# Value products of attention behind every second unit, block 2's latent half ahead of the shift, and a variance sum moved to VectorE

## The chip, the cores and the metric

One core of one Trainium2 chip runs the whole program in one launch. The metric is the device time in microseconds (us); the number that counts is the median of three runs. TensorE (PE in the profile) does the matrix products, VectorE (DVE) and ScalarE (ACT) the elementwise work, GpSimd (POOL) some sums and descriptors, SyncE (SP) issues most transfers.

## The reference

Two layers of a hybrid backbone over 512 latent and 256 context tokens of width 1024. A modulation vector (6 x 1024 wide, from `silu(c) @ w_ada`) gives shift, scale and gate.

```python
h = modulate(rmsnorm(x, g_mix[l]), sh1, sc1)
hc = modulate(rmsnorm(ctx, g_mix[l]), csh1, csc1)
q, k, v, u = split_in(h @ w_in[l])                 # 8 query heads, 2 key/value heads, and the conv columns u
a_out = latent_attention(q, k, v, k_c, v_c, attn_sink[l])   # window of +/-128 tokens, all context keys, a sink
cv_out = conv_module(u, w_dw[l], b_dw[l], ln_g[l], ln_b[l]) # GLU, 31 taps, layernorm, silu
x = x + gt1 * merge_groups(a_out, cv_out, g_attn_out[l], g_conv_out[l], w_out[l])
h2 = modulate(rmsnorm(x, g_ffn[l]), sh2, sc2)
x = x + gt2 * swiglu(h2, w_gate_up[l], w_down[l])
...
mu = jnp.mean(xf, axis=-1, keepdims=True)          # layernorm of the conv branch
var = jnp.mean(jnp.square(xf - mu), axis=-1, keepdims=True)
y = (xf - mu) * lax.rsqrt(var + EPS)
```

Context tokens go through the same weights in the first layer; in the second only their keys and values are needed.

## The kernel before, in words

Activations lie with features on the 128 partitions and tokens along the free axis. Every weight and activation is split into a high and a low part, and each product is made of three matrix products (high x high, high x low, low x high). ScalarE makes the high part of a 128x1024 weight block (line 989), VectorE the low part (line 1327). The order on each engine is written out by hand and tied together by semaphores; there is no planner.

**The start (lines 860 to 905).** The first phase, `u`, has eight blocks of output columns (four pairs). The RMS root is applied after the product, so products can start with `gain * x`. TensorE first makes the scale half of the first modulation group (`first_unit(0, k)`, eight units of four products each, fed by 1 MB transfers that hold two units), with filler products (`keep_busy`) between. Then it makes the latent half of block 0 and block 1 (`latent_part`, 512 columns), with the eight units of the shift half between, turns the shift's row (`first_turn(1)`), waits for the shift (`sh_ok`), and makes the context half of both blocks (`context_part`, 256 columns and the two shift columns). Blocks 2 to 7 are made whole by `gemm_block` in `phase`, with the units of the second modulation group (`ada_unit`, 1 MB each, two buffers) between, and two conv tiles. The loads of these stand on SP's queue, in order, each behind a semaphore that says that its buffer is free.

**The normalisation of the conv branch.** ScalarE squares the centred tiles (`dev_ok`), GpSimd adds the four squares (lines 1921 to 1925), TensorE turns the sum (`var_tokens`, in block 3 of phase `qkv`), VectorE reduces it and inverts ScalarE's root (`diagonal`), and TensorE broadcasts it in block 4.

**Attention (lines 735 to 850, 1070 to 1110, 1424 to 1505).** A unit is one head of one 128-query block; four units make a group (one KV head, one query block), which has 4, 5, 5, 4, 2 or 2 key tiles by its query block (in the second layer 4, 5, 5, 4). In unit n TensorE turns the probabilities of n (`turn`, line 800, into the one bank pair `PTB`), makes the scores of unit n + 4 (line 787, two banks in turn), and part of the value products of the group before (`values`, line 815: two products of 64 output rows, at two places of the array). ScalarE copies the turned probabilities (`prob_turned`, line 1090) and then takes the exponential of unit n + 3 (line 1080). VectorE takes the maximum of unit n + 4 and divides unit n + 2. Three waits matter here:

```python
pe.wait_ge(pt_ok, u)       # turn(n): ScalarE has copied the turned probabilities of n - 1
pe.wait_ge(exp_ok, u - 1)  # scores(n + 4): ScalarE has read the scores of n + 2
if m * GRP // len(qs[q][2]) == n % GRP:   # key tile m of the group before goes into this unit
```

Before, the key tiles of a group of four lie one in each unit, of a group of five in units 0, 0, 1, 2, 3, of a group of two in units 0 and 2.

## Time and profile before

| | us |
|---|---|
| median of 3 runs (1519.5 to 1524.03) | 1522.55 |
| the profiled execution, its own time | 1523.91 |
| its span in the trace | 1522.1 |
| TensorE busy | 1492.6 (98%) |
| VectorE busy | 891.8 (59%) |
| ScalarE busy | 529.0 (35%) |
| share of the chain that ended last: TensorE, VectorE, ScalarE, transfers | 89%, 6%, 1%, 2% |

A timeline row gives start, length, engine, line, operation, output and inputs, and in brackets the idle time ahead and what ended it. An instruction's length reaches into the next one's, since they overlap: what one costs is the distance from its start to the start of the next.

### The profile page before, as it was taken

The page shows a single profiled execution, that of the slowest core. Times are in us where ns is not written, and L with a number is a line of the kernel's source. Part 1 is how long each engine was busy: PE and PEld are TensorE (multiplying, and loading weights), DVE is VectorE, ACT ScalarE, POOL GpSimd, SP SyncE. Part 2 cuts the span into 40 slices and gives each one's busy share as a digit, 9 for nine tenths or more (in the row PEclk, how much of TensorE's full clock was granted, in tenths as well). Part 3 has the DMA queues.
Part 4 walks back from the last instruction along what each step waited for, and adds up shares of the span by engine and source line. Part 5 has one row for each costly group of instructions (what it writes and reads, how often), then busy time and mean ns, then how long its engine had stood idle before and what let it go on. Part 6 is the DMA issues. An engine that isn't in the chain of part 4 may idle for free.

```text
span 1522.1 us, 22743 instructions
## 1 busy us (share of the span) xinstructions
PE 1492.6 (98%) x8962; PEld 1231.3 (81%) x8962; DVE 891.8 (59%) x1335; ACT 529.0 (35%) x810; POOL 104.5 (7%) x149
## 2 busy tenths in 40 slices
PE   8999999999999999999999999999999999999998
PEld 5766776688888888888888889777689888888887
DVE  4756779677667325765853466768887433333334
ACT  4302368634222112222122244138844322222234
POOL 0133200040000000000000000520030000000000
PEclk9999999999999999999999999999999999999999
DMA  9493600023332123323432123520023333333322
GB/s 375 167 263 96 237 27 29 1 70 111 119 143 96 56 91 144 124 110 138 154 109 69 45 67 111 150 64 15 29 70 98 97 96 97 97 96 97 97 83 97
DMA packets 40855, 161.15 MB, mean 106 GB/s; under 512 B 5584, under 2 KB 6992, under 8 KB 34640
## 3 DMA queue, kind: packets, MB, share of 16 engines
q1 hardware_dynamic: 36848, 148.72, 29.0%
q0 software_dynamic: 3936, 11.45, 2.8%
q8 instruction: 48, 0.79, 0.2%
q14 instruction: 23, 0.19, 0.0%
HBM read 149.76 MB, written 2.10 MB: 100 GB/s over the span
## 4 chain that ended last, share of the span: by engine, by line
PE 89%; DVE 6%; issue 2%; DMA 2%; ACT 1%; SPq 0%; ACTq 0%; DVEq 0%
PE banks L624 75%; PE banks L653 3%; PE banks L800 2%; PE banks L787 2%; PE banks L815 2%; PE banks L536 1%; DMA ada_raw<-in_w_ada 1%; PE banks L679 1%; DVE neg_max L1445 1%; PE banks L545 1%; DVE ada_sum_context L1412 0%; DVE x L1421 0%; PE banks L589 0%; DMA ada_first<-in_w_ada_first 0%; PE banks L853 0%
## 5 line engine op out<-in xcount | busy, mean ns | idle before, releaser
L624 PE MATMUL banks<-h_both,w_high 128*128 128x258 f32 (+2 forms) x2432 | 492.9, 324 | 4.2 <-DVE tmp L1373 1.7
L989 ACT ACTIVATE w_high<-raw 128x1024 fp32r<-128x1024 f32 (+2 forms) x182 | 186.2, 1023 | 706.5 <-PE banks L624 645.7
L624 PEld LDWEIGHTS banks<-h_both,w_high 128*128 128x128 f32 x2432 | 364.3, 189 | 51.8 <-issue 15.1
L1327 DVE TENSOR_TENSOR w_low<-raw,w_high 128x1024 fp32r<-128x1024 f32 (+2 forms) x182 | 216.4, 1189 | 246.9 <-ACT w_high L989 243.5
L624 PE MATMUL banks<-h_both,w_low 128*128 128x512 f32 (+1 forms) x1216 | 293.7, 323 | 0.0
L624 PEld LDWEIGHTS banks<-h_both,w_low 128*128 128x128 f32 x1216 | 187.2, 189 | 17.7
L624 PE MATMUL banks<-h_normal_low,w_high 128*128 128x512 f32 x304 | 118.3, 389 | 0.0
L624 PE MATMUL banks<-h_normal_high,w_high 128*128 128x512 f32 x304 | 118.3, 389 | 0.0
L624 PE MATMUL banks<-h_normal_high,w_low 128*128 128x512 f32 x304 | 118.3, 389 | 0.0
L1372 DVE COPY shift_product<-banks 128x2 f32<-128x2 f32 x78 | 12.3, 158 | 169.3 <-PE banks L624 160.2
L624 PE MATMUL banks<-ff_high,w_high 128*128 128x512 f32 x352 | 90.2, 337 | 0.0
L624 PE MATMUL banks<-ff_high,w_low 128*128 128x512 f32 x352 | 89.8, 336 | 0.0
L624 PE MATMUL banks<-ff_low,w_high 128*128 128x512 f32 x352 | 89.8, 336 | 0.0
L1373 DVE TENSOR_TENSOR tmp<-banks,inv_root 128x768 f32<-128x768 f32 (+1 forms) x78 | 69.1, 886 | 0.0
L624 PE MATMUL banks<-ff_last_high,w_high 128*128 128x512 f32 x176 | 68.5, 389 | 0.0
L624 PE MATMUL banks<-ff_last_low,w_high 128*128 128x512 f32 x176 | 68.5, 389 | 0.0
L624 PE MATMUL banks<-ff_last_high,w_low 128*128 128x512 f32 x176 | 68.5, 389 | 0.0
L624 PEld LDWEIGHTS banks<-h_normal_high,w_low 128*128 128x128 f32 x304 | 57.1, 188 | 12.0
L624 PEld LDWEIGHTS banks<-h_normal_low,w_high 128*128 128x128 f32 x304 | 57.1, 188 | 11.8
L1445 DVE TENSOR_REDUCE neg_max<-banks 128x1 f32<-128x513 f32 (+2 forms) x80 | 54.9, 687 | 19.9 <-PE banks L787 19.3
L624 PEld LDWEIGHTS banks<-h_normal_high,w_high 128*128 128x128 f32 x304 | 57.1, 188 | 11.7
L1421 DVE SCALAR_TENSOR_TENSOR x<-banks,mod,x 128x512 f32<-128x512 f32 (+1 forms) x96 | 60.3, 656 | 10.5 <-PE banks L624 10.5
(218 smaller groups left out, 2058.6 us busy)
## 6 DMA issues: line engine op xcount, KB each, us to landing
raw<-in_w_gu SPq DMA_DIRECT2D x88, 512.0 KB, 3.5
ada_raw<-in_w_ada SPq DMA_DIRECT2D x20, 1024.0 KB, 5.6
raw<-in_w_dn SPq DMA_DIRECT2D x32, 512.0 KB, 3.5
raw<-in_w_mix SPq DMA_DIRECT2D x28, 512.0 KB, 4.6
ada_in_ff<-in_w_ada SPq DMA_DIRECT2D x12, 1024.0 KB, 5.6
raw<-in_w_out SPq DMA_DIRECT2D x16, 512.0 KB, 3.5
ada_first<-in_w_ada_first SPq DMA_DIRECT2D x7, 1024.0 KB, 11.9
raw<-in_w_dn SPq DMA_DIRECT2D x16, 384.0 KB, 3.0
```

The source lines that it names most:

```text
L536: last = mm(bank[32 * q:32 * q + 32, ADA, :], cond[:, k, :], tile[:, 512 * q:512 * q + 512], start=(k == 0), stop=(k == DT - 1), tile_posi ...
L545: last = mm(bank[32 * q:32 * q + 32, ADA, D // 4 * v:D // 4 * v + D // 4], cond[:, k, :], tile[:, k % 2, D // 4 * q:D // 4 * q + D // 4], ...
L624: last = mm(bank[:, 2 * slot + bk, to:to + b - a], weights[w][:, k0_w + k, :], rhs[:, k0_rhs + k, a:b], start=(k == 0 and n == 0), stop=(k ...
L653: last = mm(bank[QC * q:QC * q + QC, BC + bk, 0:b - a], wD[:, j, g, QC * q:QC * q + QC], zr[j][:, q, SH * g + a:SH * g + b], start=(g == 0 ...
L787: last = mm(wide[:, at:at + w], lhs, rhs, start=in_bank[m] not in in_bank[:m], stop=in_bank[m] not in in_bank[m + 1:], skip_group_check=True)
L800: last = nc.tensor.transpose(wide[:, 512 * PTB + P * m:512 * PTB + P * m + P], pr[:, P * m:P * m + P], ident[:])
L815: last = mm(bank[HD * odd:HD * odd + HD, BC + n % 2, 0:2 * P], V[:, keys[m], HD * g:HD * g + HD], PT[:, n % 2, m, 2 * odd:2 * odd + 2, :]. ...
L989: last = f(wH[j][:, at, :], raw[j][:, at, :], ACT.Copy)
L1327: last = tt(wL[j][:, at, :], raw[j][:, at, :], f32(wH[j][:, at, :]), ALU.subtract)
L1373: tt(like(tmp[slot]), src, like(rs), ALU.mult).then_inc(slot_free[slot], 1)
L1421: last = stt(out=xt, in0=bank[:, 2 * slot + (a >= N), 0:b - a], scalar=mod[:, layer, bass.ds(t + gate * DT, 1), v], in1=xt, op0=ALU.mult, ...
L1445: nc.vector.reduce_max(nmax[:, c:c + 1], score_place(u, qs[q][2]), AX.X, negate=True).then_inc(max_ok, 1)
```

## The change

Three parts.

1. `VALUES_AT` puts the value products behind units 1 and 3 of a group alone: of four key tiles two and two, of five three and two, of two both behind unit 3.
2. At the start the loads come in another order (the params, three weight tiles of the scale half, then the first block and the identity); fewer filler products; the latent half of block 2 is made ahead of the shift in banks 6 and 7, from a third pair of buffers (`w_first`); the context squares and the shift come behind the context's high and low parts on ScalarE and VectorE; the context half of three blocks follows the shift. Five of the eight units of the second modulation group get buffers of their own, in regions that are idle then, and are loaded in advance; the units go behind blocks 2, 2, 3, 3, 4, 5, 6, 7 in place of 2, 3, 3, 4, 5, 6, 6, 7.
3. In the second layer VectorE adds the squares for the variance, behind its low part in block 1 of `qkv`, in place of GpSimd; its `diagonal` and ScalarE's root come ahead of the weight split of block 2 in place of behind it, and the root's table is loaded early.

```diff
+        VALUES_AT = {2: (3, 3), 4: (1, 1, 3, 3), 5: (1, 1, 1, 3, 3)}
...
-                            if m * GRP // len(qs[q][2]) == n % GRP:
+                            if VALUES_AT[len(qs[q][2])][m] == n % GRP:
                                 values(q, m)
...
             if name == "u":
-                at = (2, 3, 3, 4, 5, 6, 6, 7)
+                at = (2, 2, 3, 3, 4, 5, 6, 7)
...
+        for k, (tile, landed, count, free) in enumerate((
+                (ada_raw[:], ada_in[0], 16, DT), (ada_in_u[:], ada_in[1], 16, DT), (zr_flat[1], ada_more[0], 16, DT),
+                (zr_flat[0], ada_more[1], 16, DT), (ada_in_cv[:], ada_more[2], 16, DT),
+                (ada_raw[:], ada_in[0], 32, DT + 1), (ada_in_u[:], ada_in[1], 32, DT + 2), (ada_raw[:], ada_in[0], 48, DT + 6))):
+            ADA_PLACES[1, k] = (tile, landed, count, (ada_mm, free))
...
                 first_unit(0, k)
                 if k in (1, 3, 5):
-                    keep_busy(3)
-            keep_busy(1)
+                    keep_busy(2 if k == 1 else 1)
...
-            first_unit(1, 4)
-            first_unit(1, 5)
-            stat_tokens((0, "n1"), NB)
-            first_unit(1, 6)
-            first_unit(1, 7)
-            stat_broadcast((0, "n1"), NB)
+            pe.wait_ge(w_low, 3)
+            for k in range(DT):
+                latent_part(2, k, (0, 1, 2), k == 0, k == DT - 1)
+                if k == 1:
+                    stat_tokens((0, "n1"), NB)
+                elif k == 3:
+                    first_unit(1, 4)
+                    first_unit(1, 5)
+                elif k == 4:
+                    stat_broadcast((0, "n1"), NB)
+                elif k == 6:
+                    first_unit(1, 6)
+                    first_unit(1, 7)
+            pe.wait_ge(rs_ok, 1)
             first_turn(1)
             keep_busy(2)
 
             pe.wait_ge(sh_ok, 1)
-            for k in range(DT):
-                pe.wait_ge(h_ok, k + 1)
-                context_part(0, k)
...
+            for t in range(3):
+                for k in range(DT):
+                    if t == 0:
+                        pe.wait_ge(h_ok, k + 1)
+                    context_part(t, k)
...
             for k in range(DT):
                 act.wait_ge(xc_in[k // 4], 16)
                 high(k, x[:, k, :], gains(0, 0, True, k)[1:])
+            copy_root((0, "n1"), N)
+            for k in range(DT):
                 square("xc", 0, k, x[:, k, N:T], N)
+            act.wait_ge(ada_mm, DT)
+            f(ada_row[0][:, D // 4:D // 2], bank[:, ADA, D // 4:D // 2], ACT.Copy).then_inc(ada_rowed, 1)
             root((0, "n1c"), LB)
...
+                    if t == 2 and not context:
+                        diagonal((layer, "var"), blocks)
                     split_low(layer, "qkv", t // 2, t % 2)
+                    if t == 1 and not context:
+                        for k in range(1, CT):
+                            dve.wait_ge(dev_ok, CT * layer + k + 1)
+                            made = tt(ssum[:, 0:width], ssum[:, 0:width] if k > 1 else cv[:, 0, 0:width],
+                                      cv[:, k, 0:width], ALU.add)
```

**TensorE in attention.** Before, in the first layer, a stretch in which a group of five key tiles has its probabilities turned (line 800), the scores of units to come are made (787) and the values of the group before follow (815; `x2` is one key tile):

```order
L800 MATMUL banks<-ident,prob 128x128 x5
L787 MATMUL banks<-k_stacked,q_stacked 128x256 x4
L787 MATMUL banks<-maskb,identb 128x128
L787 MATMUL banks<-sink_rows,ones_bf 128x1
L815 MATMUL banks<-probT,v_tokens 64x256 x4
L800 MATMUL banks<-ident,prob 128x128 x5
L787 MATMUL banks<-k_stacked,q_stacked 128x256 x4
L787 MATMUL banks<-maskb,identb 128x128
L787 MATMUL banks<-sink_rows,ones_bf 128x1
L815 MATMUL banks<-probT,v_tokens 64x256 x2
L800 MATMUL banks<-ident,prob 128x128 x5
L787 MATMUL banks<-k_stacked,q_stacked 128x256 x4
L787 MATMUL banks<-maskb,identb 128x128
```

The same stretch in the changed kernel (turn 841, scores 828, values 856):

```order
L841 MATMUL banks<-ident,prob 128x128 x5
L828 MATMUL banks<-k_stacked,q_stacked 128x256 x4
L828 MATMUL banks<-maskb,identb 128x128
L828 MATMUL banks<-sink_rows,ones_bf 128x1
L841 MATMUL banks<-ident,prob 128x128 x5
L828 MATMUL banks<-k_stacked,q_stacked 128x256 x4
L828 MATMUL banks<-maskb,identb 128x128
L828 MATMUL banks<-sink_rows,ones_bf 128x1
L856 MATMUL banks<-probT,v_tokens 64x256 x6
L841 MATMUL banks<-ident,prob 128x128 x5
L828 MATMUL banks<-k_stacked,q_stacked 128x256 x4
L828 MATMUL banks<-maskb,identb 128x128
```

Each turn had scores and values in front of it before; now the turns of a group's units 1 and 3 come right behind scores, and the values of three and two key tiles stand together in front of the turns of units 2 and 0.

**TensorE at the start.** Before, the end of block 1's latent half (679), the last units of the shift half (545), the tokens' turn (589) and broadcast (606), the turn of the shift's row (558), filler (853) and the context half (685):

```order
L679 MATMUL banks<-h_both,w_low 128x512
L679 MATMUL banks<-h_both,w_high 128x512
L679 MATMUL banks<-h_both,w_low 128x512
L545 MATMUL banks<-ada_first,cond 32x256 x8
L589 MATMUL banks<-ident,ssum 128x128 x4
L545 MATMUL banks<-ada_raw,cond 32x256 x8
L606 MATMUL banks<-ident,per_tok 128x128 x4
L558 MATMUL banks<-ident,act_out 128x128 x2
L853 MATMUL banks<-cond,ones 128x256 x2
L685 MATMUL banks<-h_both,w_high 128x258 x2
L685 MATMUL banks<-h_both,w_low 128x258
L685 MATMUL banks<-h_both,w_high 128x258 x2
```

The same place in the changed kernel (units 578, tokens' turn 622, broadcast 640, latent part 720, row turn 591, filler 894, context part 726):

```order
L640 MATMUL banks<-ident,per_tok 128x128 x4
L720 MATMUL banks<-h_both,w_high 128x512 x2
L720 MATMUL banks<-h_both,w_low 128x512
L720 MATMUL banks<-h_both,w_high 128x512 x2
L720 MATMUL banks<-h_both,w_low 128x512
L578 MATMUL banks<-ada_raw,cond 32x256 x8
L720 MATMUL banks<-h_both,w_high 128x512 x2
L720 MATMUL banks<-h_both,w_low 128x512
L591 MATMUL banks<-ident,act_out 128x128 x2
L894 MATMUL banks<-cond,ones 128x256 x2
L726 MATMUL banks<-h_both,w_first 128x258 x9
L622 MATMUL banks<-ident,ssum 128x128 x2
```

The latent products of block 2 now lie between the broadcast and the row's turn, and the context half starts with the weights of `w_first`.

**VectorE in block 1 of `qkv`, second layer.** Before, from the product's scaling (1373) over the low part (1327) to the rotation (1532 to 1542) and the next product:

```order
L1373 TENSOR_TENSOR tmp<-banks,inv_root 128x512
L1327 TENSOR_TENSOR w_low<-raw,w_high 128x1024
L1531 STREAM_SHUFFLE shift_product_rotated<-shift_product 128x2
L1532 STREAM_SHUFFLE diagonals<-tmp 128x512
L1536 SCALAR_TENSOR_TENSOR diagonals<-diagonals,shift_product_rotated,sinT 128x512
L1539 SCALAR_TENSOR_TENSOR tmp<-tmp,shift_product,cosT 128x512
L1542 TENSOR_TENSOR tmp<-tmp,diagonals 128x512
L1372 COPY shift_product<-banks 128x2
L1373 TENSOR_TENSOR tmp<-banks,inv_root 128x512
L1327 TENSOR_TENSOR w_low<-raw,w_high 128x1024
```

The same place in the changed kernel (low part 1387, adds 1740, reduction 1410, inverse 1413):

```order
L1434 TENSOR_TENSOR tmp<-banks,inv_root 128x512
L1387 TENSOR_TENSOR w_low<-raw,w_high 128x1024
L1740 TENSOR_TENSOR ssum<-conv 128x512
L1740 TENSOR_TENSOR ssum<-ssum,conv 128x512 x2
L1592 STREAM_SHUFFLE shift_product_rotated<-shift_product 128x2
L1593 STREAM_SHUFFLE diagonals<-tmp 128x512
L1597 SCALAR_TENSOR_TENSOR diagonals<-diagonals,shift_product_rotated,sinT 128x512
L1600 SCALAR_TENSOR_TENSOR tmp<-tmp,shift_product,cosT 128x512
L1603 TENSOR_TENSOR tmp<-tmp,diagonals 128x512
L1433 COPY shift_product<-banks 128x2
L1434 TENSOR_TENSOR tmp<-banks,inv_root 128x512
L1410 TENSOR_REDUCE token_sum<-banks 128x4
L1413 RECIPROCAL per_tok<-per_tok 128x4
L1387 TENSOR_TENSOR w_low<-raw,w_high 128x1024
```

Three adds are new ahead of the rotation, and the reduction and the inverse, which came behind the low part of block 2, now come ahead of it.

## Rows read from the trace of the kernel before

**Rows 1.** Timeline, TensorE at the start: start, length, engine, line, operation, [idle before].

```profile
8.23 1.93 PE L545 MATMUL banks<-ada_first,cond 128*32 128x256 f32 x16 [1.77 <-DMA ada_first<-in_w_ada_first]
...
17.23 1.07 PE L545 MATMUL banks<-ada_first,cond 128*32 128x256 f32 x16
...
35.38 1.07 PE L545 MATMUL banks<-ada_first,cond 128*32 128x256 f32 x16
...
38.86 0.38 PE L558 MATMUL banks<-ident,act_out 128*128 128x128 f32 x2
...
50.99 0.93 PE L624 MATMUL banks<-h_both,w_high 128*128 128x512 f32 x4 [0.62 <-DVE tmp L1373]
...
59.48 1.06 PE L536 MATMUL banks<-ada_raw,cond 128*32 128x512 f32 x8
```

**Rows 2.** Timeline, VectorE at the start.

```profile
41.18 0.42 DVE L1337 TENSOR_TENSOR ssum<-ssum,sq 128x256 f32<-128x256 f32 x1
```

**Rows 3.** All transfers, the one shift tile that lies in `ada_raw` (issued at 14.30).

```profile
ada_raw<-in_w_ada_first SPq DMA_DIRECT2D x1, 1024.0 KB, 19.3
```

**Rows 4.** Timeline, TensorE ahead of the first conv tile.

```profile
102.07 1.06 PE L536 MATMUL banks<-ada_raw,cond 128*32 128x512 f32 x8 [2.60 <-DMA ada_raw<-in_w_ada]
```

**Rows 5.** Busy time by stretch, attention: stretch, length, busy (count) by engine, clock, DMA.

```profile
216.34:290.72 74.38, 70.03 (x490) 46.02 (x491) 60.93 (x155) 59.50 (x143) 0.00 (x0) 1.00 0.05 15
232.93:259.62 26.69, 24.25 (x164) 15.41 (x162) 25.11 (x65) 23.69 (x59) 0.00 (x0) 1.00 0.14 41
1048.97:1102.00 53.03, 51.86 (x386) 36.18 (x386) 44.40 (x103) 44.11 (x95) 0.00 (x0) 1.00 0.07 21
```

**Rows 6.** Timeline, TensorE, units of a group of five key tiles, first layer.

```profile
261.61 0.76 PE L800 MATMUL banks<-ident,prob 128*128 128x128 f32 x5
262.13 0.83 PE L787 MATMUL banks<-k_stacked,q_stacked 128*128 128x384 f32 x4
...
263.01 0.65 PE L815 MATMUL banks<-probT,v_tokens 128*64 128x256 f32 x4
263.59 0.76 PE L800 MATMUL banks<-ident,prob 128*128 128x128 f32 x5
...
268.81 1.08 PE L815 MATMUL banks<-probT,v_tokens 128*64 128x256 f32 x8
269.83 0.76 PE L800 MATMUL banks<-ident,prob 128*128 128x128 f32 x5
```

**Rows 7.** Timeline, ScalarE in the first of these units.

```profile
262.47 0.70 ACT L1090 ACTIVATE probT<-banks 128x640 f32<-128x640 f32 x1 [0.50 <-PE banks L800]
263.07 0.79 ACT L1080 ACTIVATE prob<-banks,neg_max 128x641 f32<-128x641 f32 x1
263.75 0.20 ACT L1080 ACTIVATION_READ_ACCUMULATOR prob<-banks,neg_max 128x1 f32 x1
```

**Rows 8.** Timeline, TensorE, units with no value products, second layer.

```profile
1044.19 0.63 PE L800 MATMUL banks<-ident,prob 128*128 128x128 f32 x4
...
1045.65 0.66 PE L800 MATMUL banks<-ident,prob 128*128 128x128 f32 x4
1046.29 0.86 PE L787 MATMUL banks<-k_stacked,q_stacked 128*128 128x384 f32 x4
```

**Rows 9.** Timeline, ScalarE in the same units.

```profile
1044.86 0.60 ACT L1090 ACTIVATE probT<-banks 128x512 f32<-128x512 f32 x1 [0.42 <-PE banks L800]
...
1046.03 0.20 ACT L1080 ACTIVATION_READ_ACCUMULATOR prob<-banks,neg_max 128x1 f32 x1
```

**Rows 10.** Timeline, TensorE around block 4 of `qkv`, second layer.

```profile
1020.94 0.97 PE L624 MATMUL banks<-h_both,w_high 128*128 128x512 f32 x4 [0.75 <-DVE w_low L1327]
...
1023.51 0.65 PE L606 MATMUL banks<-ident,per_tok 128*128 128x128 f32 x4 [1.24 <-DVE per_tok L1353]
```

**Rows 11.** Timeline, VectorE ahead of that block.

```profile
1014.72 1.78 DVE L1539 SCALAR_TENSOR_TENSOR tmp<-tmp,shift_product,cosT 128x512 f32<-128x512 f32 x1
...
1024.89 0.75 DVE L1539 SCALAR_TENSOR_TENSOR tmp<-tmp,shift_product,cosT 128x512 f32<-128x512 f32 x1
```

More of the change, by code:

```diff
@@ L295, in hybrid_backbone @@
         ada_in = [sem(f"ada_in{j}") for j in range(2)]
[L296 removed]
+        first_in = [sem(f"ada_first_in{j}") for j in range(DT + 1)]
+        ada_more = [sem(f"ada_more_in{j}") for j in range(3)]
         wd_in = [sem(f"w_conv_in{j}") for j in range(2)]
@@ L1168, in _ @@
                 for t in range(V_TILE):
+                    if t == 2 and not context:
+                        root((layer, "var"), blocks)
                     split_high(layer, "qkv", t // 2, t % 2)
@@ L1173, in _ @@
                             f(cv[:, k, 0:width], z[:, k, 0:width], ACT.Square).then_inc(dev_ok, 1)
-                    if t == 2:
+                        f(psums[:, 0:1], eps[:], ACT.Sqrt)
+                    if t == 2 and context:
                         root((layer, "var"), blocks)
@@ L1367, in shift_low, with scale_product @@
                 last.then_inc(sh_ok, 1)
-            def scale_product(slot, context):
-                src, like = product(slot, context)
-                nc.vector.tensor_copy(shifted[:, slot, :], shift_cols(slot, context))
+            def scale_product(slot, context, place=None):
+                place = slot if place is None else place
+                src, like = product(place, context)
+                nc.vector.tensor_copy(shifted[:, slot, :], shift_cols(place, context))
                 tt(like(tmp[slot]), src, like(rs), ALU.mult).then_inc(slot_free[slot], 1)
@@ L1636, in u_pair @@
                     dve.wait_ge(gemm, 2 * use + 1)
-                    scale_product(0, context)
+                    scale_product(0, context, BC // 2 if (layer, i) == (0, 1) else 0)
                     if i:
@@ L1669, in _ @@
                         scale_deviation(layer, width)
+                    if t == 2 and not context:
+                        diagonal((layer, "var"), blocks)
                     split_low(layer, "qkv", t // 2, t % 2)
+                    if t == 1 and not context:
[3 more added lines that the diff above has]
+                                      cv[:, k, 0:width], ALU.add)
+                            if k < CT - 1:
+                                chain.link(made)
+                        made.then_inc(conv_sum, 1)
                     if t > 1:
@@ L1674, in _ @@
                         scale_deviation(layer, width)
-                    if t == 2:
+                    if t == 2 and context:
                         diagonal((layer, "var"), blocks)
```

159 lines of the change are left out of this document (97 added, 62 removed).

## The prediction, made before the changed kernel ran

> **What bounds the kernel now.** I read the page first, for who is busy and who ends the chain: TensorE, nearly throughout. So a change counts here in two ways only: it takes TensorE's time away, or it takes away a wait of TensorE; work on another engine counts where TensorE waits for it. Then the timeline of TensorE at the start, where the reader is to see that its products are held by transfers and by filler [rows 1], and the one transfer wait behind it, 2.60 us [rows 4]. Then attention by stretch: from the first value products on, TensorE is busy in 70.03 of 74.38 us in the first layer and in 51.86 of 53.03 in the second [rows 5], but in 232.93 to 259.62 the other two engines carry extra work and TensorE has 2.4 us idle. Then the timelines of TensorE and ScalarE inside a unit [rows 6 to 9], since part 1 moves work between units; last the waits at block 4 of `qkv` in the second layer, which part 3 is about [rows 10, 11].
>
> **Part 1, value products.** What they cost: one key tile between scores and the next turn takes 263.59 - 263.01 = 0.58 us, two take 269.83 - 268.81 = 1.02 [rows 6]. So a further tile costs 0.44, and going over to the half-width products and back costs 0.14 a visit. Groups of four and five key tiles go from four visits to two, groups of two from two to one; without the last group of each layer, which makes its values at the end, that is 19 visits less in the first layer and 14 in the second. 33 x 0.14 = 4.6 us less work on TensorE.
>
> What they hide: turn(n + 1) writes the banks that ScalarE copies turned probabilities n out of. With five key tiles ScalarE begins the copy 262.47 - 261.61 = 0.86 behind the turn's start and its exponential 0.60 behind that [rows 6, 7]. Before, TensorE has 0.52 of turn, 0.88 of scores and 0.58 of values, 1.98 in all, and never waits. Without the values it could turn again at 1.40. How long it must wait is seen where a group's first units have no values: with four key tiles the next turn comes 1045.65 - 1044.86 = 0.79 behind the start of a 0.60 copy [rows 8, 9], so 0.19 behind its end. With the 0.70 copy that makes 0.86 + 0.70 + 0.19 = 1.75. A second wait follows: scores n + 5 need the bank of n + 3, whose exponential ends 263.75 + 0.20 - 263.07 = 0.88 behind its start [rows 7], so at 0.86 + 0.60 + 0.88 = 2.34; TensorE goes on 1046.29 - (1046.03 + 0.20) = 0.06 later [rows 8, 9], at 2.40. So a pair of units takes 2.40 + 0.88 of scores + 1.02 of values = 4.30 us, where it took 3.96. With three value tiles it takes 4.74, with the shorter scores of a coming group of four 0.14 less. That the two waits are real and of this size is not a guess: the unit from 1044.19 shows both, turn 1.46 later and scores at 2.10.
>
> By groups, in us, after (before): five tiles turned, five to come, 8.6 (7.95), four times; five and four to come 8.65 to 8.95 (7.75 in two groups, some 8.6 in the two where ScalarE's copies of the last queries already stop TensorE); four and four 7.95 (7.45); four and five 7.95 (7.5); the groups of two at the first layer's end 7.2 and 5.75 (6.3 and 5.0); each layer's last group 0.5 more. From 232.93 to 259.62, where VectorE and ScalarE are the slower ones [rows 5], I put 0.4. The sum is 79.3 for 74.38 and 56.9 for 53.03: 8.8 us lost. From below, the cost is bounded by the waits not showing at all, -4.6; from above by waits in the covered stretch as well, 8.8 + 3. I take 8.8, since both waits are read from the very units that lack values.
>
> **Part 2, the start.** Transfers first: the last tile of the shift half, with 11.2 MB issued up to it, lands at 14.30 + 19.3 = 33.6 [rows 3]; the first tile, with 1.7 MB, at 8.2 (the wait before 8.23 [rows 1]). That is 0.37 MB per us. The scale half needs the same 4.7 MB as before, so its last unit can't be done before 8.2 + 3.0/0.37 + 0.5 = 16.8; filler held it to 17.23 + 1.0 = 18.2. Gain 1.4 to 1.5. Everything to the end of block 1's latent half keeps its order and comes that much earlier: 33.9 for 35.4. Behind it TensorE has block 2's latent part: a whole block takes 59.48 - 50.99 = 8.49 [rows 1], by columns (512 of 770) 5.65 of it; with four units at 0.5, turn and broadcast 1.1 it ends at 42.6. (The last shift tile now has 12.7 MB up to it and lands at 37.9, no wait.)
>
> Next is the shift. ScalarE and VectorE now put it behind the context's parts, the root's copy (bank ready at 39.5, copied at 40) and eight squares and adds at 0.42 [rows 2], so 3.9 with the ends: the row is copied at 44.3, and from the row's turn to the first context product it took 40.7 - 38.86 = 1.9, of which I take 1.3, as the tiles are there already. Context products start at 45.6. Three halves at 2.85 and 0.7 of turns end at 54.9: block 2 is complete at 54.9 for 59.5, 4.6 us gained, though TensorE idles for 2 us ahead of the shift. From there the order holds the same products and units, all tiles of five units long loaded, so the 2.60 goes too [rows 4]: 7.2 us. Could VectorE, with ten conv taps for each pair, now be the late one? It idles 12 us before the low part at 115 and 9 before 142; no. GpSimd's shifted copies hang on the same products as before and move with them. The bounds: context products between 44.5 and 48, so 2.3 to 5.8, plus 2.6: 4.9 to 8.4 us gained.
>
> **Part 3, the variance.** TensorE waits 0.75 for the low part of block 4 and 1.24 for the inverse root [rows 10]. The second goes. But three adds of 512 columns, some 2.1 us, come ahead of the rotation on VectorE; the rotation gets shorter, since its 1.78 us instruction, beside GpSimd's adds, took 0.75 elsewhere [rows 11], with two more like it 1.5 in all. The reduction and ScalarE's root then stand ahead of the low part of block 4, which comes 0.8 later. Gained 0.3 (from -0.5, if the low part slips by the adds' whole length, to +1.5).
>
> On that row the Trainium skill says (GPSIMD Engine Reference, Specifications) that GpSimd and VectorE share their SBUF interfaces when VectorE has two SBUF inputs; the trace agrees, 1.78 against 0.75 [rows 11].
>
> **Sum.** 8.8 - 7.2 - 0.3 = 1.3 us slower. The profiled execution took 1523.91, so 1525.2 in its terms; the median stands 1.36 below it, so I forecast 1523.8 us. Two changes of 7 to 9 us that cancel.
>
> **Rivals.**
> A: the waits of part 1 don't show and only the visits' cost goes: -4.6 - 7.2 - 0.3, 1510.4 us. For it: TensorE is busy nearly throughout, and the drain is seen in the rows. Against it: the units from 1044.19. The Trainium skill (TensorEngine Tiling (Array Packing), Key Properties) says that changing the tiling mode drains TensorE. By that rule alone part 1 can only gain.
> B: the waits show but cost as much as the visits give back, because ScalarE starts the copy sooner when nothing overlaps it: part 1 at 0, 1515 us. For it: the visit's 0.14 and a wait of 0.33 are close. Against it: the 0.86 are TensorE's own turn and a hand-over.
> C, slower: TensorE's clock falls at the start. The pause ahead of the context products (42.6 to 45.6, with two fillers in it) and the missing fillers are the place; the first units took 1.93 us where later ones took 1.07 [rows 1], half speed, after a pause of 1.8. If the clock falls there, 9.3 us of context products take up to twice as long: 4 to 9 lost, so 1528 to 1533, say 1530. It decides from 3 us of lost time on. Against it: pauses of 1.5 us at 20 to 22 left later products at full speed.
> The Trainium skill (TensorE: Matmul & The Clock Gate, Why this matters for your kernels) warns of gaps of some 3 us between bursts of matmuls; the estimated pause lies at it with the fillers left out, and below it with them. By that rule the time would be C's.
>
> **Chances.** Forecast 0.66, its own range 1519 to 1528 (part 1 from 5 to 10, part 2 from 5 to 8.4); A 0.11; B 0.10; C 0.13. A measurement of this kernel can tell 0.3% from no change, 4.6 us: below 1518.0 is faster, above 1527.1 slower. Faster: A, most of B, a little of the forecast, 0.21. Slower: C and the forecast's upper end, 0.17. Same: 0.62. The range 1515 to 1529 leaves out A and half of C.
>
> **What would show it.** In attention, rows of TensorE's turn that wait for ScalarE's copy, twice in a group, and scores that wait for the exponential, with pairs of 4.3 us; the stretch of 53.0 at 57. At the start, the first conv tile 7 us earlier, no transfer wait, block 1's latent half ending near 34. In the second layer the wait for the inverse root gone and the one for the low part longer. I am wrong if attention is not longer, or if the conv tile comes less than 5 us earlier.

## The result: 0.3% slower, and the profile after

The changed kernel takes 1527.96 us (median of 16 runs, 1526.19 to 1530.39), the kernel before in the same runs 1523.89. The ratio is 1.0031, 95% interval 1.0023 to 1.0039: 4 to 5 us slower. The forecast was 1523.8 against a median of 1522.55, so +1.3. The profiled execution has a span of 1526.7 us, where the kernel before had 1522.1.

The lines of the program moved: what was L800 (turn) is L841 now, L787 (scores) L828, L815 (values) L856, L1090 (ScalarE's copy) L1145, L1080 (exponential) L1135, L624 (blocks) L658.

**Attention.** Busy time by stretch of the changed kernel, to be held against [rows 5]: stretch, its length, busy time (count) of TensorE, its weight loads, VectorE, ScalarE and GpSimd, granted clock, DMA share, GB/s. Both rows run from the first five-tile turn to the start of the last value products, the first in layer 0 (the first layer), the second in layer 1.

```profile
211.06:290.27 79.21, 68.45 (x483) 47.48 (x483) 60.56 (x154) 59.14 (x141) 0.00 (x0) 1.00 0.05 14
1049.74:1105.90 56.16, 51.17 (x378) 37.22 (x378) 44.44 (x102) 43.47 (x93) 0.00 (x0) 1.00 0.07 20
```

TensorE is busy 1.6 us less in the first stretch (68.45 for 70.03), and the stretch is 4.8 us longer (79.21 for 74.38): work went and waiting came. (Of the 1.6, 0.9 did not go but moved behind the end of the stretch, see below.) Who ended the waiting is in the answer on the turns (name, count, shortest, median and longest duration, first and last start; then idle time ahead of them by releaser):

```profile
L841 PE MATMUL banks<-ident,prob x120: 272/273/329, 211.1 to 289.0; 128*128 128x128 f32 x120
...
  ACT probT L1145: 8.1, 20
```

Twenty times a turn waited for ScalarE's copy, 8.1 us in all; before it was once, 0.4 us. Inside a pair of five-tile units, TensorE (start, length, engine, line, operation, [idle before]), for [rows 6]:

```profile
260.55 0.77 PE L841 MATMUL banks<-ident,prob 128*128 128x128 f32 x5
261.07 0.83 PE L828 MATMUL banks<-k_stacked,q_stacked 128*128 128x384 f32 x4
...
262.26 0.74 PE L841 MATMUL banks<-ident,act_out 128*128 128x128 f32 x5 [0.23 <-ACT probT L1145]
262.95 0.85 PE L828 MATMUL banks<-k_stacked,q_stacked 128*128 128x384 f32 x4
...
263.86 1.08 PE L856 MATMUL banks<-probT,v_tokens 128*64 128x256 f32 x8
264.87 0.77 PE L841 MATMUL banks<-ident,prob 128*128 128x128 f32 x5
```

and ScalarE beside it, for [rows 7]:

```profile
261.41 0.70 ACT L1145 ACTIVATE probT<-banks 128x640 f32<-128x640 f32 x1 [1.15 <-PE banks L841]
262.01 0.79 ACT L1135 ACTIVATE prob<-banks,neg_max 128x641 f32<-128x641 f32 x1
262.69 0.20 ACT L1135 ACTIVATION_READ_ACCUMULATOR prob<-banks,neg_max 128x1 f32 x1
```

The next turn comes 262.26 - 260.55 = 1.71 behind the turn (forecast 1.75), 0.15 behind the copy's end. The scores behind it come at 2.40, 0.06 behind the exponential's end at 262.89 (forecast 2.40). The pair takes 264.87 - 260.55 = 4.32 (forecast 4.30, before 3.96).

**What the forecast did not have.** The tail of layer 0's attention:

```profile
287.86 0.41 PE L841 MATMUL banks<-ident,prob 128*128 128x128 f32 x2 [0.63 <-ACT probT L1145]
288.89 0.41 PE L841 MATMUL banks<-ident,prob 128*128 128x128 f32 x2 [0.62 <-DVE act_out L1516]
289.93 0.41 PE L841 MATMUL banks<-ident,act_out 128*128 128x128 f32 x2 [0.62 <-ACT probT L1145]
290.27 3.40 PE L856 MATMUL banks<-probT,v_tokens 128*64 128x256 f32 x16
```

Four key tiles of value products (x16) now stand at the end, where there were two. Eight products (two tiles) took 1.08 us at 263.86; sixteen take 3.40 here. The granted clock (the third figure from the end of a row) says why:

```profile
290.27:293.60 3.33, 3.33 (x17) 1.59 (x17) 0.42 (x1) 1.67 (x2) 0.00 (x0) 0.55 0.02 5
45.31:49.04 3.73, 3.73 (x17) 3.37 (x18) 1.00 (x7) 0.00 (x0) 0.00 (x0) 0.61 1.02 422
17.43:21.00 3.57, 3.56 (x9) 2.34 (x10) 2.05 (x7) 2.40 (x4) 0.00 (x0) 0.52 1.06 398
```

0.55 is nearly the lower level, 1.2 GHz, throughout. Just ahead of it, in the same kernel, TensorE stood still three times in four units, for 0.62 us each, at the full clock.

**The start.** The second and third rows above are the start: the clock was down there twice. The stretch from 17.43, behind waits of 1.59, 0.66 and 0.59 us, cost nothing by its end: block 1's latent half ends at 33.99, as forecast. TensorE's timeline, for [rows 1]:

```profile
42.60 0.40 PE L720 MATMUL banks<-h_both,w_low 128*128 128x512 f32 x1
45.31 0.66 PE L591 MATMUL banks<-ident,act_out 128*128 128x128 f32 x2 [2.31 <-ACT act_out L1188]
45.76 1.91 PE L894 MATMUL banks<-cond,ones 128*128 128x256 f32 x4
47.12 1.95 PE L726 MATMUL banks<-h_both,w_first 128*128 128x258 f32 x9
...
56.99 1.07 PE L569 MATMUL banks<-ada_raw,cond 128*32 128x512 f32 x8
...
97.67 10.51 PE L687 MATMUL banks<-z_shifted,w_conv 128*32 128x512 f32 x128
```

Block 2 is done at 56.99 (forecast 54.9, before 59.48), and the first convolution tile starts at 97.67, 5.3 us earlier than before (102.95); the forecast had 7.2. Of the transfer wait of 2.60 [rows 4] nothing is left.

**The variance.** TensorE at block 4 of `qkv` in layer 1, for [rows 10], and VectorE's rotation, for [rows 11]:

```profile
1022.75 0.97 PE L658 MATMUL banks<-h_both,w_high 128*128 128x512 f32 x4 [1.52 <-DVE w_low L1387]
...
1023.91 0.60 PE L640 MATMUL banks<-ident,per_tok 128*128 128x128 f32 x4
```

```profile
1017.38 0.75 DVE L1600 SCALAR_TENSOR_TENSOR tmp<-tmp,shift_product,cosT 128x512 f32<-128x512 f32 x1
```

One wait of 1.52 for the low part in place of 0.75 and 1.24: the inverse root is ready when TensorE comes to it. The rotation's 1.78 is 0.75.

### The profile page after: what moved, and what is told of

It is laid out like the page before. It is cut to its first block, busy times and chain, and to the rows that moved or that the text cites. A ratio compares the mean times of both kernels' runs of the same rounds, so it can differ in the third digit from the quotient of the medians.

```text
span 1526.7 us, 22719 instructions
## 1 busy us (share of the span) xinstructions
PE 1488.0 (97%) x8950; PEld 1231.8 (81%) x8950; DVE 893.2 (59%) x1337; ACT 530.6 (35%) x812; POOL 99.4 (7%) x146
## 4 chain that ended last, share of the span: by engine, by line
PE 89%; DVE 5%; ACT 3%; issue 2%; DMA 1%; SPq 0%; ACTq 0%; DVEq 0%
PE banks L658 75%; PE banks L687 3%; PE banks L841 2%; PE banks L856 2%; PE banks L828 2%; ACT probT L1145 1%; PE banks L569 1%; PE banks L720 1%; DMA ada_first<-in_w_ada_first 1%; PE banks L726 1%; DVE neg_max L1506 1%; DVE ada_sum_context L1473 0%; DVE x L1482 0%; ACT prob L1135 0%; PE banks L622 0%
## 5 line engine op out<-in xcount | busy, mean ns | idle before, releaser
L658 PE MATMUL banks<-h_both,w_high 128*128 128x512 f32 (+1 forms) x2400 | 485.2, 324 | 4.5 <-DVE w_low L1387 1.5
L658 PEld LDWEIGHTS banks<-h_both,w_high 128*128 128x128 f32 x2400 | 358.9, 189 | 51.2 <-issue 14.4
L658 PE MATMUL banks<-h_both,w_low 128*128 128x258 f32 (+2 forms) x1200 | 289.2, 322 | 0.0
L658 PEld LDWEIGHTS banks<-h_both,w_low 128*128 128x128 f32 x1200 | 184.6, 189 | 17.4
L658 PE MATMUL banks<-h_normal_low,w_high 128*128 128x512 f32 x304 | 118.3, 389 | 0.0
L658 PE MATMUL banks<-h_normal_high,w_high 128*128 128x512 f32 x304 | 118.3, 389 | 0.0
L658 PE MATMUL banks<-h_normal_high,w_low 128*128 128x512 f32 x304 | 118.3, 389 | 0.0
L658 PE MATMUL banks<-ff_high,w_high 128*128 128x512 f32 x352 | 90.2, 337 | 0.0
L658 PE MATMUL banks<-ff_low,w_high 128*128 128x512 f32 x352 | 89.8, 336 | 0.0
L658 PE MATMUL banks<-ff_high,w_low 128*128 128x512 f32 x352 | 89.8, 336 | 0.0
L658 PE MATMUL banks<-ff_last_high,w_high 128*128 128x512 f32 x176 | 68.5, 389 | 0.0
L658 PE MATMUL banks<-ff_last_low,w_high 128*128 128x512 f32 x176 | 68.5, 389 | 0.0
L658 PE MATMUL banks<-ff_last_high,w_low 128*128 128x512 f32 x176 | 68.5, 389 | 0.0
L658 PEld LDWEIGHTS banks<-h_normal_low,w_high 128*128 128x128 f32 x304 | 57.1, 188 | 11.9
L658 PEld LDWEIGHTS banks<-h_normal_high,w_low 128*128 128x128 f32 x304 | 57.1, 188 | 11.9
L658 PEld LDWEIGHTS banks<-h_normal_high,w_high 128*128 128x128 f32 x304 | 57.1, 188 | 11.7
```

The source lines that it names most:

```text
L658: last = mm(bank[:, 2 * slot + bk, to:to + b - a], weights[w][:, k0_w + k, :], rhs[:, k0_rhs + k, a:b], start=(k == 0 and n == 0), stop=(k ...
```

## The experiments

Two questions: what each part is worth by itself, and why the start gave 5.3 where 7.2 were forecast. Theory: part 1 costs what TensorE waits for ScalarE's copy and exponential; part 2 gives 5 to 7 us; part 3 about nothing. Rivals: the attention got longer for another reason (moved transfers, the clock), or the waits cost nothing.

| kernel | median, us | kernel before beside it | ratio and 95% interval |
|---|---|---|---|
| `old_values` | 1518.05 | 1523.39 | 0.9963, 0.9948 to 0.9978 |
| `only_values` | 1535.06 | 1523.39 | 1.0065, 1.0047 to 1.0083 |
| `filler` | 1526.80 | 1523.39 | 1.0021, 1.0009 to 1.0034 |
| `one_visit` | 1537.84 | 1523.39 | 1.0093, 1.0070 to 1.0116 |
| `short_copy` | 1519.52 | 1525.02 | 0.9969, 0.9959 to 0.9979 |
| `early_shift` | 1515.23 | 1525.02 | 0.9935, 0.9922 to 0.9948 |
| `fillers_start` | 1517.02 | 1525.02 | 0.9946, 0.9929 to 0.9963 |
| `no_variance` | 1517.54 | 1525.02 | 0.9957, 0.9940 to 0.9973 |
| `kept_busy` | 1514.51 | 1522.93 | 0.9943, 0.9929 to 0.9957 |
| `early_again` | 1513.67 | 1522.93 | 0.9939, 0.9925 to 0.9953 |
| `after_again` | 1528.22 | 1522.93 | 1.0033, 1.0021 to 1.0044 |

Where attention is compared, it is from the first five-tile turn to the tokens' turn in layer 0 (before: 216.34 to 291.74, 75.40 us) and to the last turn in layer 1 (1048.97 to 1100.63, 51.66).

**1. Parts 2 and 3 alone** (`old_values`).

```diff
-                            if VALUES_AT[len(qs[q][2])][m] == n % GRP:
+                            if m * GRP // len(qs[q][2]) == n % GRP:
```

> The changed kernel with the value products put back into every unit, so parts 2 and 3 alone. If part 1 costs what its two waits cost (theory), the 11 us by which the two attentions got longer come back, and 5.6 us are gained at the start and in the variance: 1517 to 1519 us, ratio to the kernel before 0.9960, attention of layer 0 at 74.4 us between the turns that rows 5 name and that of layer 1 at 53.0. Rival, the start causes the rest (the transfers moved at the start, or the clock, slow attention down too): the attentions stay longer by 2 us or more and the time is above 1521.

Measured 1518.05, ratio 0.9963. Layer 0 takes 75.40, layer 1 51.65, within a hundredth what they took before. The start does not slow attention. That rival is out.

**2. Part 1 alone** (`only_values`): the diff of 1 the other way, in the kernel before.

> The kernel before with part 1 alone. Theory, the waits for ScalarE's copy and exponential and a half-speed end of layer 0's attention: +10 to +11.5 us, 1534 to 1535.5 us, ratio 1.0070, and again the last value products of layer 0 at half speed (16 in 3.3 us). If that half-speed end comes from the shifted start and not from the placement, +9 us. Rival A of the prediction (only the saved visits count): 1519.

Measured 1535.06, 1.0065. Layer 0 takes 82.74 and layer 1 55.92 (the changed kernel: 82.54 and 55.61). The last sixteen value products are at half speed again:

```profile
294.95:298.49 3.54, 3.54 (x18) 1.72 (x17) 0.42 (x1) 1.67 (x2) 0.00 (x0) 0.52 0.02 5
```

The two single-part kernels give 1523.39 x (0.0065 - 0.0037) = 4.3 us together, and the change gave 4 to 5: the parts add up.

**3. Idle work in the wait** (`filler`).

```diff
                                 values(q, m)
+                        if n % GRP in (0, 2):
...
+                            mm(bank[:, BC + g1 % 2, 2 * P:4 * P], ones[:], cond[:]..., ..., skip_group_check=True)
```

> The changed kernel with one idle product of 256 columns, fp32, on TensorE in each unit that has lost its value products, from the second group of a layer on: 36 of them, about 0.45 us each, 16 us more work for TensorE. Theory (TensorE stands still there for ScalarE, 0.35 us at the turn and the rest at the scores): the filler lies in the wait, time within 2 us of the changed kernel's, and if the end of layer 0's attention then keeps the full clock 1.5 us less: 1526 to 1529 us. Rival (TensorE is the bound in those units and the pairs are long for another reason): +14 to +16 us, 1543.

Measured 1526.80, 1.2 us below the changed kernel's median for 36 products more (the ratios' intervals overlap, so the two times are the same as far as they can be told apart). The lines of the turns and of the fillers, from 205 to 312 us (busy us, mean ns, idle ahead by releaser):

```profile
L841 PE MATMUL banks<-ident,prob 128*128 128x128 f32 x124 | 20.5, 283 | 2.7 <-DVE prob L1522 0.9 <-ACT probT L1151 0.7 <-DVE act_out L1522 0.6
L892 PE MATMUL banks<-cond,ones 128*128 128x256 f32 x44 | 13.6, 391 | 0.0
```

x44 is 22 products of two passes each, at 0.47 us a product (1.89 for four of them in experiment 7). In layer 0 alone some 10 us of matrix work that computes nothing went in and cost nothing, and layer 1 takes 55.62 for 55.61: TensorE really stands still in those units. Its last sixteen value products take 1.95 us, and layer 0 takes 81.06, 1.48 less than in the changed kernel. That is the price of the half-speed tail.

**4. One visit a group** (`one_visit`): `VALUES_AT = {2: (3, 3), 4: (3, 3, 3, 3), 5: (3, 3, 3, 3, 3)}`.

> The changed kernel with all value products of a group in the last unit of the next group: one visit where it has two, three units of four without cover. Theory (each uncovered unit takes 1.75 us by ScalarE's copy with five key tiles, 1.46 to 1.6 with four): +0.3 to +0.5 us a group, 18 groups, +5 to +9: 1533 to 1537 us. Rival (a visit costs 0.14 us and the waits are no cost): -0.14 x 15 = -2 us, 1526.

Measured 1537.84, just above the expected span, but for a largely wrong reason. A five-tile group in the clean stretch:

```profile
262.81 0.74 PE L841 MATMUL banks<-ident,prob 128*128 128x128 f32 x5 [0.24 <-ACT probT L1145]
...
266.17 0.74 PE L841 MATMUL banks<-ident,act_out 128*128 128x128 f32 x5
...
267.77 1.95 PE L856 MATMUL banks<-probT,v_tokens 128*64 128x256 f32 x16
269.64 0.77 PE L841 MATMUL banks<-ident,prob 128*128 128x128 f32 x5
```

Units of 1.71 (from the turn at 261.10), 1.68, 1.68 and 3.47, 8.54 us in all, where the changed kernel's group takes 8.63 (256.24 to 264.87): no loss. What was lost lies elsewhere, and about half of it is the clock. The granted clock was down in four stretches of this profile, of which two:

```profile
225.81:230.79 4.98, 4.98 (x30) 3.57 (x30) 3.01 (x7) 2.94 (x7) 0.00 (x0) 0.68 0.00 0
...
1112.84:1118.56 5.72, 5.72 (x37) 3.26 (x36) 0.42 (x1) 1.88 (x2) 0.00 (x0) 0.70 0.01 3
```

The second of these is the last value products of layer 1. The others are 242.73 to 246.78 at 0.59 and the start of layer 1's attention, 1048.72 to 1052.69, at 0.64. By length times the missing share of the clock the four cost an estimated 1.6, 1.7, 1.7 and 1.4 us, 6.4 in all, where the changed kernel's profile has 1.5 (its tail). The group from 219.10 takes 11.69 us (the changed kernel 9.05, at the full clock), of which 1.6 is the clock and the rest waiting, 1.57 us at one turn; the first group of two key tiles from 238.75 takes 8.03 (5.80), of which 1.7 is the clock. So this run, 10 us above the changed kernel, does not price the missing cover alone.

**5. A short copy** (`short_copy`). From the fourth group of each layer on, ScalarE copies only the first key tile of the turned probabilities; the kernel leaves the others out.

```diff
                     w = len(qs[q][2])
+                    if q >= 3:
+                        w = 1
                     act.wait_ge(pt_ps, u + 1)
                     f(PT[:, group % 2, 0:w, ...
```

> The changed kernel, where from the fourth group of each layer on ScalarE copies only the first key tile of the turned probabilities (128 columns for 512 or 640; the other tiles keep what stood there). Theory: the copy is what TensorE waits for, so without it both waits go nearly: five-tile pairs take 3.82 to 3.95 us instead of 4.30 (below the 3.96 of the kernel before, which pays two more visits), waits for the copy only in the first groups; 25 visits saved show as time: 1518 to 1521 us for the whole. Rival (waiting is set by the exponential or VectorE): pairs stay above 4.1.

Measured 1519.52, and a pair of five-tile units takes 1083.01 - 1079.12 = 3.89 us:

```profile
1079.12 0.76 PE L841 MATMUL banks<-ident,prob 128*128 128x128 f32 x5
1079.64 0.83 PE L828 MATMUL banks<-k_stacked,q_stacked 128*128 128x384 f32 x4
...
1080.43 0.71 PE L841 MATMUL banks<-ident,act_out 128*128 128x128 f32 x5
1081.09 0.85 PE L828 MATMUL banks<-k_stacked,q_stacked 128*128 128x384 f32 x4
...
1081.99 1.08 PE L856 MATMUL banks<-probT,v_tokens 128*64 128x256 f32 x8
1083.01 0.77 PE L841 MATMUL banks<-ident,prob 128*128 128x128 f32 x5
```

The turn is followed at 1.31, with no wait for the copy, now 0.28 us. The second scores still wait 0.14 (0.66 behind their turn, where the first come at 0.52), for an exponential that ends at 1081.03. Without that the pair would be 3.75, against 3.96 with a visit more. So a saved visit is worth an estimated 0.21 us, more than the 0.14 of the forecast: the scores ahead of it end 0.1 later too (0.90 to the values, 0.79 to a turn). The gain was there, and the copy ate it.

**6. The shift earlier** (`early_shift`): on `old_values`, ScalarE's copy of the shift row and VectorE's shift columns go behind the fourth of the eight context squares and adds.

```diff
             for k in range(DT):
                 square("xc", 0, k, x[:, k, N:T], N)
-            act.wait_ge(ada_mm, DT)
-            f(ada_row[0][:, D // 4:D // 2], bank[:, ADA, D // 4:D // 2], ACT.Copy).then_inc(ada_rowed, 1)
+                if k == 3:
+                    act.wait_ge(ada_mm, DT)
+                    f(ada_row[0][:, D // 4:D // 2], bank[:, ADA, D // 4:D // 2], ACT.Copy).then_inc(ada_rowed, 1)
...
-                    if (t, k) == (0, 2):
+                    if (t, k) == (0, 6):
...
```

> Parts 2 and 3 alone, and in the start ScalarE's copy of the shift row and VectorE's shift columns moved from behind the eight squares and adds of the context to behind the fourth of them (context sums turned later, behind products 6 and 4 of the next two halves). Theory: the context products wait for this chain alone; the row is copied at 42.4 instead of 44.8 us, they start near 44.8 instead of 47.1, TensorE's pause of 2.3 us goes and with it the half speed of the fillers and of the first nine context products (0.7 us): block 2 done 2.5 to 3.2 us earlier, 1515 us against 1518. Rival: the sums and inverse roots of the context, now a microsecond later, are late next and the block's scaling holds block 3: 0 to -1 us.

Measured 0.9935 (0.9963 for parts 2 and 3 as they are), some 4 us by the ratios, 3 us by the profile. TensorE has no pause:

```profile
43.59 0.38 PE L591 MATMUL banks<-ident,act_out 128*128 128x128 f32 x2
43.81 1.03 PE L894 MATMUL banks<-cond,ones 128*128 128x256 f32 x4
44.72 2.79 PE L726 MATMUL banks<-h_both,w_first 128*128 128x258 f32 x21
...
94.67 10.51 PE L687 MATMUL banks<-z_shifted,w_conv 128*32 128x512 f32 x128
```

The convolution tile starts at 94.67, 3.0 earlier than in the changed kernel, and nothing is late next.

**7. Fillers in the pause only** (`fillers_start`): `keep_busy(4)` ahead of `first_turn(1)`, on `old_values`.

> Parts 2 and 3 alone, and four idle products (fp32, 256 columns) on TensorE in the pause ahead of the shift row's turn, 1.9 us of them at full speed in a pause of 2.3. Theory: the pause is what put TensorE at half speed behind it; the two fillers behind the turn take 1.0 us instead of 1.9, the first nine context products 1.1 instead of 1.8, and the context products start at 46.8: 0.8 to 1.0 us less, 1517. Rival: the half speed of that stretch has nothing to do with the pause (the fillers are at half speed too, since they are at such a duration wherever they stand): 0 to +1 us.

Measured 1517.02, 0.9946. The two fillers behind the turn take 1.03 us instead of 1.91 and nine context products 1.35 instead of 1.95:

```profile
43.59 1.89 PE L894 MATMUL banks<-cond,ones 128*128 128x256 f32 x8
46.07 0.41 PE L591 MATMUL banks<-ident,act_out 128*128 128x128 f32 x2 [0.59 <-ACT act_out L1189]
46.31 1.03 PE L894 MATMUL banks<-cond,ones 128*128 128x256 f32 x4
47.23 1.35 PE L726 MATMUL banks<-h_both,w_first 128*128 128x258 f32 x9
```

So with work in the pause the clock stayed up: 1.00 from 46.07 to 48.55. One profile does not prove that the pause had brought it down, though, for the same pause did not do so every time. In `filler`, whose start is that of the changed kernel:

```profile
44.71 0.41 PE L591 MATMUL banks<-ident,act_out 128*128 128x128 f32 x2 [2.33 <-ACT act_out L1194]
...
45.87 1.34 PE L726 MATMUL banks<-h_both,w_first 128*128 128x258 f32 x9
```

Of the thirteen profiles here, seven have this pause of 2.3 us. Five of them show the lower clock behind it; `filler` and `short_copy` do not. None of the six without the pause shows it there. So the pause seems to bring the half speed in most executions, and not in all. Where it did not, the first convolution tile starts at 95.83 and 95.98, 7.1 and 7.0 us earlier than in the kernel before (0.6 and 0.4 of it were there already at the unit of 27.97).

The context products of `fillers_start` came no earlier than 47.23, since this execution was 0.75 late by then (the unit of 27.97 starts at 28.72): its clock was at 0.50 from 16 to 22 us, where the changed kernel's was back at full by 21. The times alone can't tell this kernel from `old_values`: the intervals overlap.

**8. Part 2 alone** (`no_variance`): the squares added on GpSimd and the root behind block 3, as before.

> Part 2 alone: part 3 is undone as well (GpSimd adds the squares of layer 1's deviations again, the root behind block 3). Theory: the inverse root's wait of 1.24 us is back and block 4's wait at 0.75: +0.3 us, 1518.4. Rival: part 3 is worth the whole of the wait that it takes away, +1.2. Both lie within what the times can tell, so the stretch from block 3 to the first turn is read.

Measured 0.9957, no different. The profile has both waits back, and half speed behind the second:

```profile
1015.21 0.97 PE L658 MATMUL banks<-h_both,w_high 128*128 128x512 f32 x4 [0.67 <-DVE w_low L1384]
...
1017.77 1.04 PE L640 MATMUL banks<-ident,per_tok 128*128 128x128 f32 x4 [1.23 <-DVE per_tok L1410]
1018.46 1.63 PE L658 MATMUL banks<-h_both,w_high 128*128 128x512 f32 x4
```

From the mean's product to the first scores it takes 1031.34 - 1001.74 = 29.60 us, with part 3 (`old_values`) 1029.77 - 1001.34 = 28.43. From the broadcast's row (1017.77) to those scores it takes 13.57; in the kernel before, with the same two waits and the full clock, 1036.19 - 1023.51 = 12.68. So 0.9 of the 1.17 is the clock, and part 3 is worth the other 0.3. The kernel before gives the same: 1036.19 - 1007.46 = 28.73 for the whole stretch, 0.3 more than with part 3, at the full clock in both. That is one profile against another; the times can't show 0.3 us.

**9. Does the half speed belong to the program?** Three runs: fillers in four waits of each attention on `early_shift` (`kept_busy`), and `early_shift` and the changed kernel once more.

```diff
                 scores(2)
+                pe.wait_ge(exp_ok, unit0 + 2)
+                mm(bank[:, BC, 2 * P:4 * P], ones[:], cond[:]..., start=True, stop=True, skip_group_check=True)
...
                         scores(3)
+                        mm(bank[:, SMALL, 2 * P:4 * P], ones[:], cond[:]..., start=True, stop=True, skip_group_check=True)
...
+                    if n >= len(order) - GRP and n % GRP in (1, 3):
...
+                        mm(bank[:, BC + group_index[layer, last_q] % 2, 2 * P:4 * P], ones[:], cond[:]..., ...)
```

> The kernel with the early shift, and one idle product (fp32, 256 columns, 0.5 us) in four waits of each attention: ahead of the first turn (0.86 us), ahead of the fifth scores (0.59), and behind two units of the last group (0.62 and 0.53). Theory: such waits are where TensorE falls to half speed in some executions and not in others (1.4 us at the start of layer 1's attention in five of ten profiles, 0.9 to 1.5 us at the end of layer 0's in three), so its time is 0.5 to 1.5 us below that of the early shift in the same runs and varies less, and its profile shows neither. Rival: the fillers hold up the scores that follow them: 0.5 to 1 us more.

> The kernel with the early shift once more, beside the kept-busy one. Theory: ratio 0.9935 again; its profile may or may not show the half speed at the start of layer 1's attention and at the end of layer 0's, both of which its first profile showed. Rival, the half speed belongs to the program: the same two stretches at half speed.

> The changed kernel once more, for a second profile. Theory: the last value products of layer 0 at half speed (16 in 3.3 us) are no part of the change: they take 1.95 us in some executions, and then the attention takes 81.1 us from the first five-tile turn to the tokens' turn instead of 82.5. Rival, they belong to the placement (the other kernel with that placement in layer 0's last groups had them too): 3.3 us again.

Measured 0.9943 for `kept_busy` and 0.9939 for `early_again`: the fillers gain nothing that can be measured. Its profile shows the full clock in both attentions, as expected, but so does that of `early_again`, without them. `early_shift` had shown half speed at the start of layer 1's attention and at the end of layer 0's:

```profile
1036.39:1041.44 5.05, 4.98 (x25) 4.46 (x26) 3.33 (x12) 3.22 (x8) 0.00 (x0) 0.66 0.00 0
282.45:284.33 1.88, 1.88 (x8) 0.77 (x8) 0.00 (x0) 1.25 (x1) 0.00 (x0) 0.51 0.04 9
```

The same program showed neither the second time: the four first turns of layer 1 took 1039.66 - 1031.96 = 7.70 us for 9.08. There it comes and goes. The tail of layer 0 with the new placement is another matter; in `after_again`:

```profile
289.69 3.29 PE L856 MATMUL banks<-probT,v_tokens 128*64 128x256 f32 x16
```

It was at half speed in all three profiles that had this placement with the full copy and no filler, at full speed in one of each with fillers, one visit or a short copy (1.95 each). With the old placement it was at half speed in one of seven (`early_shift`). I had expected the opposite. Three profiles are few, but here it looks like part of the placement; why is not shown.

## Why the prediction was nearly right

**The mechanism of part 1 was right, its size short.** Both waits were found where the forecast put them, 1.71 and 2.40 for 1.75 and 2.40, pairs of 4.32 for 4.30. The stretches came out at 79.21 for 79.3 and 56.16 for 56.9. The failing step is "each layer's last group 0.5 more". The sum stopped at the start of the last value products, and with the new placement two key tiles more lie behind that point: 0.87 us in layer 0 (1.95 for 1.08 at full speed) and 0.86 in layer 1 (2.81 for 1.95). That makes 4.83 + 3.13 + 0.87 + 0.86 = 9.7 for 8.8. In layer 1 two errors nearly cancel by luck: the stretch came out 0.7 below the forecast and the tail that it left out is 0.86. And 1.5 us of half speed behind three waits of 0.62 was in no term. By the runs, part 1 is 1523.39 x 0.0065 = 9.9 us (7 to 13). A second error sits inside and did no harm: a visit is worth some 0.21 us and not 0.14, but since the waits set the pair, its price didn't enter the sum.

**Rivals A and B fall.** A needed no waits. Fillers of some 10 us in layer 0 at no cost show that they are real, and the short copy shows what they wait for. B needed a copy that starts sooner; it starts 261.41 - 260.55 = 0.86 behind the turn, as before. The rule of the Trainium skill (TensorEngine Tiling (Array Packing), Key Properties), that a change of tiling mode drains the array, agrees with these rows, where a visit costs some 0.21 us. It says that a visit costs something, and not what the visit covers.

**Part 2 was the term that was mis-sized:** 5.3 us by the convolution tile for 7.2. "Context products start at 45.6": they start at 47.12. Block 2 came 2.1 us late, in four pieces. ScalarE copied the row at 44.80 for 44.3, 0.5. Turn and fillers took 47.12 - 45.31 = 1.81 at half speed, where experiment 7 has 47.23 - 46.07 = 1.16, 0.65. The next nine products and the tokens' turn took 1.92 for its 1.32, 0.6. The rest, 0.4, is a hand-over that I had put too short. The end of block 1's latent half (33.99 for 33.9) and of all latent parts (43.0 for 42.6) were right, and so was the 2.60. Of the four pieces the two largest, 1.25 us, are the clock. The two profiles that kept it have context products at 45.87 and 46.03, block 2 done at 55.15 and 55.30 and 7.1 and 7.0 us gained, with the help of a start that was 0.6 and 0.4 earlier. So most of what part 2 lacked is that its sum left the clock out.

**Rival C happened, in small, and in most profiles.** It was priced at 4 to 9 us with a chance of 0.13. Behind the pause of 2.31 us the granted clock was 0.61, but over 3.7 us, not over all 9.3 of the context products, and it cost the 1.25 just named. The argument against it (pauses of 1.5 us at 20 to 22 left later products at full speed) is true of the kernel before, where the clock is 1.00 there, but says nothing of a longer pause. The Trainium skill (TensorE: Matmul & The Clock Gate, Why this matters for your kernels) warns of pauses of some 3 us between bursts. Here 2.31 was enough in five profiles of seven, and in the tail of layer 0 three of 0.62. C's other place, the missing fillers, shows too: nine of the eleven profiles of kernels with the new start have the lower clock from about 16 us on, for 3 to 7 us, and the two with the old start don't. Whether it is the fillers that are missed there was not tested. In the changed kernel that cost nothing; in `early_shift` and `fillers_start`, where it lasted longer, the unit of 27.97 comes 0.75 us later. One reading behind C is not borne out: in 8.23 to 10.16, where it saw half speed, the profile of the kernel before has a granted clock of 1.00, so only the length of 1.93 us speaks for it.

**Part 3 was right:** 0.3 us, one wait longer (1.52), one gone, the rotation's 1.78 down to 0.75.

The sum: 9.9 by the runs for part 1, less 5.6 for parts 2 and 3 (1523.39 x 0.0037), is 4.3; the forecast had 8.8 - 7.5 = 1.3. By the forecast's own bound of 0.3% the measured 0.31% lies at the edge between "same", which had 0.62, and "slower", which had 0.17.

The version that beats both kernels keeps the value products in every unit and the rest of the change, with the shift earlier: 0.9935 and 0.9939 of the kernel before in two sets of runs, 9 to 10 us.

## What to carry to other kernels

An instruction on the bounding engine may be cover for another engine's chain. Before bunching it, read off how long the next step would have to wait without it: a filler put in the new gap at no cost proves that the cover was needed. Where work is moved past the end of a measured stretch, the sum has to go on to a point that neither version moves across. And a pause on TensorE can be charged twice, once for itself and once for what runs at half speed behind it; whether it is differs between executions of one program, so read the granted clock before a difference of 1 to 2 us between two profiles is put down to an edit.

## What the runs showed of the hardware

- TensorE's granted clock fell to 0.5 to 0.6 for 2 to 7 us behind short pauses, and not each time. Behind one of 2.3 us at the start it fell in five of seven profiles. Behind one of 1.23 in `no_variance` it fell, behind the same one of 1.24 in the kernel before and one of 1.52 in the changed kernel it did not. Behind three of 0.62 in the tail of layer 0, with the new placement, it fell in all three profiles that had no filler, full copies and two visits. In the start of layer 1's attention (pauses of 0.86 and 0.59) it fell in five of thirteen, once with and once without in the same program, at some 1.4 us.
- A visit of TensorE to half-width products between full-width ones cost an estimated 0.21 us in fp32: 3.96 for a pair of units with two visits, 3.75 with one and the same products (3.89 measured, less a wait of 0.14).
- VectorE's instruction with two tensors in SBUF took 1.78 us beside GpSimd's adds (kernel before [rows 11] and `no_variance`) and 0.75 without them (kernel before, a block later, and the changed kernel at 1017.38).
